# One matmul of 512 columns for the high and low rows in the up tiles of the one-set FFNs

## What is computed

```python
def swiglu(h, w1, w3, w2):
    return (jax.nn.silu(h @ w1) * (h @ w3)) @ w2

x = x + 0.5 * swiglu(rms_norm(x, g), w1, w3, w2)       # twice in the first block, D_FF = 2816
x = x + 0.5 * g1x * swiglu_2(modulate(rmsnorm(x, norm_ffn1), sh1x, sc1x), w13, w2)          # second block
ctx = ctx + 0.5 * g1c * swiglu_2(modulate(rmsnorm(ctx, norm_ffn1), sh1c, sc1c), w13, w2)
```

## Time and profile before

| | |
|---|---|
| median of 3 runs | 1756.22 us (1753.88 to 1759.42) |
| the profiled execution | 1756.05 us, span 1754.3 us |
| TensorE busy, mean granted clock | 98% of the span, 0.989 |
| VectorE, ScalarE busy | 59%, 37% |
| matmuls | 13552 |
| the FFNs with one token set | about 22 to 205, 552 to 740 and 1560 to 1742 us |
| the FFN with two | about 740 to 1100 us |

### The profile page before, as it was taken

The page is one execution under the profiler, slowest core; times in us unless marked ns, Lnnn a source line. Parts: engine busy times, 40 slices in busy tenths (PEclk is TensorE's granted clock), DMA queues, the critical chain, the costliest instruction groups (busy, mean ns, idle before and its releaser), DMA issues.

```text
span 1754.3 us, 32542 instructions
## 1 busy us (share of the span) xinstructions
PE 1714.3 (98%) x13552; PEld 1562.4 (89%) x13552; DVE 1042.4 (59%) x1582; ACT 645.1 (37%) x755; POOL 4.1 (0%) x11
## 2 busy tenths in 40 slices
PE   8999999999889999999999999999999999999998
PEld 8999898777689999998888888988889799999998
DVE  6676737544287767665465464942356634767766
ACT  5333445323344333332222212422346334443332
POOL 0000000000000000000000000000000000000000
PEclk9999999999999999999999999999999999999999
DMA  7545476255824545422222222233223234545551
GB/s 267 184 180 191 178 254 241 98 229 230 313 97 174 185 174 191 167 93 100 96 96 96 96 96 96 101 116 117 79 96 108 98 145 174 187 147 188 183 184 64
DMA packets 37826, 267.76 MB, mean 153 GB/s; under 512 B 4224, under 2 KB 4480, under 8 KB 5744
## 3 DMA queue, kind: packets, MB, share of 16 engines
q1 hardware_dynamic: 37008, 263.42, 41.2%
q0 software_dynamic: 736, 3.13, 0.5%
HBM read 265.48 MB, written 1.05 MB: 152 GB/s over the span
## 4 chain that ended last, share of the span: by engine, by line
PE 91%; DVE 4%; ACT 1%; DMA 1%; issue 1%; DVEq 0%; SPq 0%; ACTq 0%
PE PS L363 25%; PE PS L364 24%; PE PS L369 24%; PE PS L678 2%; PE PS L680 2%; PE PS L679 2%; PE PS L698 2%; PE PS L1189 2%; DMA RAW<-stream 1%; DVE W_LO L357 1%; PE PS L1222 1%; PE PS L1209 1%; PE PS L446 1%; DVE NT L1689 1%; PE PS L1176 1%
## 5 line engine op out<-in xcount | busy, mean ns | idle before, releaser
L363 PE MATMUL PS<-H_HI,W_HI 128*128 128x256 f32 (+1 forms) x2112 | 642.5, 306 | 2.3 <-DVE W_LO L357 1.1
L364 PE MATMUL PS<-H_HI,W_LO 128*128 128x256 f32 (+1 forms) x2112 | 636.5, 303 | 0.0
L348 ACT ACTIVATE W_HI<-RAW 128x2048 fp32r<-128x2048 f32 x213 | 407.1, 1912 | 583.8 <-PE PS L369 534.9
L369 PE MATMUL PS<-H_LO,W_HI 128*128 128x256 f32 (+1 forms) x2032 | 617.0, 304 | 0.0
L357 DVE TENSOR_TENSOR W_LO<-RAW,W_HI 128x2048 fp32r<-128x2048 f32 x215 | 487.4, 2267 | 172.4 <-ACT W_HI L348 171.8
L363 PEld LDWEIGHTS PS<-H_HI,W_HI 128*128 128x128 f32 x2112 | 404.8, 192 | 36.3 <-issue 19.3
L364 PEld LDWEIGHTS PS<-H_HI,W_LO 128*128 128x128 f32 x2112 | 405.0, 192 | 15.3 <-issue 0.2
L369 PEld LDWEIGHTS PS<-H_LO,W_HI 128*128 128x128 f32 x2032 | 389.6, 192 | 15.1
L363 PE MATMUL PS<-HID_HI,W_HI 128*128 128x256 f32 (+1 forms) x720 | 221.3, 307 | 0.6 <-DVE HID_LO L1738 0.6
L364 PE MATMUL PS<-HID_HI,W_LO 128*128 128x256 f32 (+1 forms) x720 | 220.7, 307 | 0.0
L369 PE MATMUL PS<-HID_LO,W_HI 128*128 128x256 f32 (+1 forms) x720 | 220.7, 306 | 0.0
(11 more groups left out here) (354 smaller groups left out, 1743.6 us busy)
## 6 DMA issues: line engine op xcount, KB each, us to landing
RAW<-stream SPq DMA_DIRECT2D x249, 1024.0 KB, 4.8
XC<-xin SPq DMA_DIRECT2D x2, 512.0 KB, 5.0
XC<-xin POOLq DMA_DIRECT2D x1, 1024.0 KB, 10.6
out<-NT SPq DMA_DIRECT2D x4, 256.0 KB, 2.3
CON<-consts POOLq DMA_DIRECT2D x1, 548.0 KB, 6.1
LW<-lora POOLq DMA_DIRECT2D x1, 512.0 KB, 6.6
DFT<-dft POOLq DMA_DIRECT2D x1, 512.0 KB, 3.8
ROPE<-rope POOLq DMA_DIRECT2D x1, 256.0 KB, 2.8
```

The costliest lines, as they stand in the source:

```text
L348: nc.scalar.activation(W_HI[s % RING][:], RAW[u % RING][:], ACT.Copy).then_inc(hi_done, 1)
L363: nc.tensor.matmul(acc, w_hi, x_hi, start=first, stop=False)
L364: nc.tensor.matmul(acc, w_lo, x_hi, start=False, stop=False)
L369: return nc.tensor.matmul(acc, w_hi, x_lo, start=False, stop=last)
```

## The change

The rows H_HI and H_LO lie one behind the other in SBUF and become two views of one tile, HS. In the FFNs with one token set, an up tile (but tile 0) now does two matmuls for a block instead of three. The first has W_HI as weights and the high and low rows together as 512 columns, and its result fills the whole bank: high sum in columns 0 to 255, low sum in 256 to 511. The second has W_LO on the high rows and adds to the first half. Tile 0 keeps its three passes, and the third goes to the other half of the bank.

Both halves must then be added as they leave PSUM. ScalarE copies the gate's low half into a free half of SILU and the up tile's low half into a free half of PROD. VectorE adds the gate's high half to the first (gate_sum) and the up tile's high half to the second (up_sum). SILU then runs over SBUF, in place, after gate_sum, and PROD is the product of two SBUF tiles.

```diff
-        H_HI = sb("H_HI", [P, 2, KT, ROWS], HHI0, F32R)
-        H_LO = sb("H_LO", [P, 2, KT, ROWS], HLO0, F32R)
+        HS = sb("HS", [P, 2, 2, KT, ROWS], HHI0, F32R)
+        H_HI, H_LO = HS[:, 0], HS[:, 1]
...
+                    def tile_lo(w):
+
+                        return BK8[2 * (t % 2) + w][:, ROWS:512] if halves == 1 else tile(w)
...
-                                last = nc.tensor.matmul(tile(w), W_HI[sl][:, c:c + P], H_LO[:, 0, k], start=False, stop=(k == KT - 1))
+                                last = nc.tensor.matmul(tile_lo(w), W_HI[sl][:, c:c + P], H_LO[:, 0, k], start=(halves == 1 and k == 0), stop=(k == KT - 1))
...
+                            elif halves == 1:
+                                nc.tensor.matmul(BK8[2 * (t % 2) + w][:].rearrange("p (a n) -> p a n", a=2), W_HI[sl][:, c:c + P], HS[:, :, 0, k],
+                                                 start=(k == 0), stop=False)
+                                last = nc.tensor.matmul(tile(w), W_LO[sl][:, c:c + P], H_HI[:, 0, k], start=False, stop=(k == KT - 1))
...
+                    if halves == 1:
+                        gs = (0, 1, 1, 2)[f] * FT + t + 1
+                        A(SILU[:, t % 2, ROWS:512], BK8[2 * (t % 2)][:, ROWS:512], ACT.Copy).then_inc(S("gate_lo"), 1)
+                        act.wait_ge(psum_ready, mark + 1 if j is None else (j - j0) * 12 + mark + 1)
+                        A(PROD[:, t % 2, ROWS:512], BK8[2 * (t % 2) + 1][:, ROWS:512], ACT.Copy).then_inc(S("up_lo"), 1)
+                        act.wait_ge(S("gate_sum"), gs if j is None else (j - j0) * 2 + gs)
+                        A(SILU[:, t % 2, 0:ROWS], SILU[:, t % 2, 0:ROWS], ACT.Silu).then_inc(S("silu"), 1)
+                        return
...
+                    up_ = BK8[2 * (t % 2) + 1][:, 0:n]
+                    if halves == 1:
+                        us = (0, 1, 1, 2)[f] * FT + t + 1
+                        dve.wait_ge(S("gate_lo"), x(us, 2))
+                        V.tensor_tensor(SILU[:, t % 2, 0:ROWS], BK8[2 * (t % 2)][:, 0:ROWS], SILU[:, t % 2, ROWS:512],
+                                        ALU.add).then_inc(S("gate_sum"), 1)
+                        dve.wait_ge(S("up_lo"), x(us, 2))
+                        up_ = PROD[:, t % 2, ROWS:512]
+                        V.tensor_tensor(up_, BK8[2 * (t % 2) + 1][:, 0:ROWS], up_, ALU.add).then_inc(S("up_sum"), 1)
+                        dve.wait_ge(S("up_sum"), x(us, 2))
                     dve.wait_ge(S("silu"), x(tt + 1, 2))
                     dve.wait_ge(psum_ready, x(mark, 12))
-                    V.tensor_tensor(PROD[:, t % 2, 0:n], SILU[:, t % 2, 0:n], BK8[2 * (t % 2) + 1][:, 0:n],
+                    V.tensor_tensor(PROD[:, t % 2, 0:n], SILU[:, t % 2, 0:n], up_,
                                     ALU.mult).then_inc(S("hid_prod"), 1)
```

More of the change, by code:

```diff
@@ L359, in split_lo, with two @@
                 last.then_inc(lo_done, 1)
-        def two(acc, w_hi, w_lo, x_hi, first):
+        def two(acc, w_hi, w_lo, x_hi, first, last=False):
             nc.tensor.matmul(acc, w_hi, x_hi, start=first, stop=False)
-            nc.tensor.matmul(acc, w_lo, x_hi, start=False, stop=False)
+            return nc.tensor.matmul(acc, w_lo, x_hi, start=False, stop=last)
         def three(acc, w_hi, w_lo, x_hi, x_lo, first, last):
@@ L515, in up @@
                                 c = (w * KT + k) * P
-                                nc.tensor.matmul(tile(w), W_LO[sl][:, c:c + P], H_HI[:, 0, k], start=False, stop=False)
+                                nc.tensor.matmul(tile(w), W_LO[sl][:, c:c + P], H_HI[:, 0, k], start=False, stop=(k == KT - 1))
                     elif t == 0:
@@ L521, in up @@
                                 c = (w * KT + k) * P
-                                two(tile(w), W_HI[sl][:, c:c + P], W_LO[sl][:, c:c + P], H_HI[:, 0, k], k == 0)
+                                two(tile(w), W_HI[sl][:, c:c + P], W_LO[sl][:, c:c + P], H_HI[:, 0, k], k == 0, halves == 1 and k == KT - 1)
                     if t == 0:
```

## The result

The changed kernel takes **1746.98 us** (median of 8 runs, 1744.13 to 1749.61) where the kernel before takes 1756.12 us beside it (8 runs, 1753.10 to 1760.57): ratio 0.9942, 95% interval 0.9930 to 0.9953, so 0.58% or 9.1 us less. The forecast was 1746.4 us, with a range of 1741.5 to 1752. The profiled execution of the changed kernel took 1748.39 us, its span is 1746.6 us, 7.7 us shorter than that of before. Two executions in the third block of experiments, 3861 us of one variant and 9505 us of the kernel before, stand far outside all others and are left out of the medians.

What follows compares the result with a forecast made beforehand. TensorE, busy 98% of the span, was taken to set the loop's pace. 1756.05 us less 13.5 (matmuls) plus 3.7 (FFN ends) gave 1746.25, forecast as 1746.4 us since the profiled execution stood 0.2 under the median; range 1741.5 to 1752.

Steps and rivals of the forecast that it cites:

- Part 1: Up tiles of the one-set FFNs: a pair falls from 360.0 to 346.6 ns, 13.5 us less over 63 tiles.
- rival 2: Up tiles: a wide and a narrow matmul in turn cost 360 ns together, time 1759.9 us (or 1757.2); 7%.
- 1 ns is 1.0 us: Up tiles: 1 ns of error in the pair's price is 1.0 us of the time, the likeliest mistake.
- The sentence on the two pieces: Wide matmul's two-piece read, 16 KB apart: its cost is already in the two-set FFN's 226.6 ns.
- the forecast of a net loss: By the skill's rule the merge gives 2.5 us in all, so the change would lose about 1 us.
- Part 2: Loop of the one-set FFNs: ScalarE's 1.6 us and VectorE's 1.7 us of added work per turn are all hidden.
- D: The end of a down tile in the loop, from which the times of the ScalarE and VectorE steps are counted.
- rival 3: Loop's down tile waits each turn for the odd tile's low part, from 2.6 us over the chain: 1777 us; 7%.
- Part 3: Last down tile of each one-set FFN: TensorE waits 1.4, 1.4 and 0.9 us more, 3.7 us in sum.
- the 0.75 us: VectorE comes this late to the odd tile's sums, still splitting weights; counted at the first two FFN ends.
- Rival 1: Clock drops behind the three longer stops at FFN ends, 1.7 us each, 5.1 us, time 1751.5 us; 8%.

Runs made afterwards that it cites:

- grouped: Changed kernel with the eight wide matmuls of each up sum first and the eight narrow ones behind them, not in turn: 1743.7 us, ratio 0.9935.
- contiguous: Changed kernel with high and low rows of each k side by side in SBUF, so the wide matmul reads one piece of 512 columns: 1748.63 us, ratio 0.9962.
- before, again: The kernel before, unedited, measured and profiled a second time: 1756.61 us, ratio 1.0001.
- sums without the saving: Changed kernel's copies and sums of two bank halves, but three matmuls of 256 columns as in the kernel before: 1759.63 us, ratio 1.0008.
- only the last two FFNs: Changed kernel with the first FFN as before, the change only in the last two one-set FFNs: 1755.3 us, ratio 0.9998.
- changed, again: The changed kernel, unedited, measured and profiled a second time: 1749.2 us, ratio 0.9961.
- low sums left out: Changed kernel's wide and narrow matmuls, but ScalarE and VectorE as before the change, without copies and sums: 1745.04 us, ratio 0.9946.
- only the first FFN: Changed kernel with the change only in the first FFN, the other FFNs as before: 1751.04 us, ratio 0.9966.
- last two tiles the old way: Changed kernel with up tiles 20 and 21 of each one-set FFN by three narrow matmuls a pair, nothing to sum: 1747.42 us, ratio 0.9953.
- grouped, last two tiles the old way: Changed kernel with eight wide then eight narrow matmuls in the first twenty tiles, three narrow ones a pair in the last two: 1741.97 us, ratio 0.9924.
- flat: Changed kernel with the wide matmul's result named as one row of 512 columns, not two of 256: 1747.78 us (one run).

## Why the prediction was right, and where it wasn't

The time came out at 1746.98 where I had 1746.4, but not by my sum.

- **Part 1, the term mis-sized.** "I take 226.6 + 120.0 = 346.6 ns": measured 353.3. The saving is 6.7 ns a pair, 6.7 us over 1008 pairs, not 13.5. Both rates hold in a row of their own kind, 226.7 and 120.0 ns in the grouped kernel; what failed is that "the sum of the two is nearest", since each change of width costs on top: 6.7 ns a pair in turn, 2.5 in blocks of eight. That is halfway to rival 2. "1 ns is 1.0 us" was the warning that came true. The sentence on the two pieces held (contiguous columns changed nothing). Why a change of width costs anything stays open: pieces, the form of the result, and the added copies and sums are ruled out, and loads of W_HI behind each other too, as the last wide matmuls of a block have them and still cost 226.7.
- **The skill's rule.** The 2.5 ns of overhead in the Trainium skill ("TensorE: Matmul & The Clock Gate", "Back-to-back issue gap"), which that section gives for an isolated matmul and not for a stream with weight loads, would make the merge worth 2.5 ns a pair. The measured 6.7 lies between it and my 13.4, and the forecast of a net loss that came of it fell: the FFNs are 3.2 us shorter, and 0.8 to 1.0 us longer each with sums and no saving.
- **Part 2 held to 0.2 us.** With D at 55.95 the gate sum starts 1.2 us later (forecast 1.2), ScalarE's split 2.0 (2.1), VectorE's split ends at 6.2 (6.3), the hidden rows are ready 2.8 us after the odd tile's end at 61.60 (2.9). VectorE was 81% busy by forecast; 13.43 of 17.07 is 79%. No wait in the loop: rival 3 fell.
- **Part 3, right in kind and place, a little too dear.** Forecast 1.4, 1.4 and 0.9 us; start to start it is 1.14, 1.14 and 0.8, 3.1 us for 3.7. What was too dear is the 0.75 us by which VectorE would be late: it is 0.46 (handover about 198.13, gate sum 198.59). Tiles are longer than I had them, so VectorE is less behind.
- **Rival 1 fell.** No stretch of half clock follows the stop of the second FFN, and behind that of the last the clock is full to 1741.0, past its last down matmul. Between the stop at the first FFN's end and the next norm the clock is at 1.00; the one stretch of half clock there stands where before has it. Windows of after:

```profile
200.80:208.30 7.50, 6.31 (x52) 5.94 (x56) 5.65 (x14) 5.15 (x12) 0.00 (x0) 1.00 0.27 116
208.40:211.80 3.40, 3.40 (x20) 1.13 (x12) 2.30 (x5) 0.51 (x2) 0.00 (x0) 0.50 0.27 60
```

- **What I didn't foresee.** With the right prices my sum gives -6.7 + 3.1 = -3.6 us, some 1752.5: just above the range, and within the 0.3% that count as no change. The missing 5.5 us of the medians lie outside the FFN stages. The stops of TensorE in the first mixer, which the first FFN's shorter program sends away, are 3.4 us of them in the trace. The largest stood in the trace of before as an "issue" pause at 331.66, and the prediction's sum had no term for it. So the number was right by luck: two errors, 6.2 us too much and some 5.5 too little, cancelled.

How firm that is shows when the FFN stages of each kernel's profile are taken off its median (differences to the kernel before of the same block, us; the stops are those over 0.3 us in the first mixer that end 1.3 to 1.5 us behind a packet; kernels with a single run left out):

| kernel | such stops | median | of it outside the FFN stages |
|---|---|---|---|
| before, again | 2.7 | +0.4 | +0.4 |
| sums without the saving | 3.3 | +2.7 | +0.1 |
| only the last two FFNs | 3.3 | -1.1 | +1.0 |
| changed | 0 | -9.1 | -5.9 |
| changed, again | 0 | -7.0 | -3.8 |
| grouped | 0 | -12.5 | -5.7 |
| contiguous | 0 | -7.6 | -4.2 |
| low sums left out | 0 | -11.9 | -5.8 |
| only the first FFN | 0 | -5.3 | -4.2 |
| last two tiles the old way | 1.6 | -8.9 | -3.5 |
| grouped, last two tiles the old way | 1.3 | -14.4 | -5.6 |

Where the first FFN's part of TensorE's program is as long as before, nothing is gained outside the FFNs. Where it is shorter or longer, 3.5 to 5.9 us are, with an uncertainty of each median of 2 to 3 us. The stops that are gone explain 3.4 us or less of it. It stays open where the rest comes from, and why the half clock at 347 is in both profiles of before and in no other; the stretches of half clock move by some microseconds from run to run of one kernel. That a late packet makes the stop rests on times: in all six profiles with a stop of over 1.2 us of this kind (before, its repeat, sums without the saving, only the last two FFNs, and both with old last tiles) TensorE goes on 1.4 to 1.5 us after the packet's end, and in the changed kernel, its repeat, grouped, contiguous, flat and only the first FFN the packet comes at 328.5 to 329.3, ahead of the 64-column matmuls or under them. No run changed the packets alone.

## What to carry to other kernels

Price a mix of matmul widths as a mix: two rates, each measured in a row of its own kind, were 6.7 ns short for a pair here, half of what the merge was to save, and issuing each width in a block of eight gave back 4 of them. Where work is summed outside of PSUM to spare matmuls, do the last tiles of a loop, which have no cover, the old way; that was worth 2.2 us in three loops. And when a change alters the number of written-out instructions, compare the stages that it does not touch, since 4 to 6 us came or went there.

## What the runs showed of the hardware

- Packets of 16 KB of instructions arrive during the run, each taking 0.9 to 2.1 us (1.05 on average), one for every 126 matmuls with their weight loads in the stages between the FFNs. Where 64-column matmuls start every 16 ns, TensorE has stops of 0.4 to 2.1 us with no wait, each ending 1.3 to 1.5 us after such a packet. The longest, 2.0 us, is at the same instruction in the three kernels with as many matmuls ahead of it, and elsewhere or nowhere in the others.
- 96 matmuls of 2 columns ahead of dense ones took 15.4 us; the granted clock was 0.50 for 13.7 us, 10 of them over the tiny matmuls and 3.7 over the dense ones behind.
- A wide fp32r matmul of 512 columns with a weight load of its own costs 226.6 ns in the two-set FFN. In blocks of eight in the one-set FFN it costs 228 to 236 ns for the first five and 226.7 for the last three, and a wide and a narrow one in turn cost 353.3 ns, at the same clock of 1.00.
